# A first attention layer that turns its weights in one block, projects values later, and scores with high and low parts of q and k

## The reference, cut to what matters

```python
for i in range(DEPTH):                       # DEPTH = 2
    if i < N_A:  mix = conformer_conv(x, ...)               # layer 0
    else:                                                   # layer 1
        k_shared, v_shared = x @ kv_wk, x @ kv_wv           # 16 heads of 64
        q = x @ b_wq[j]
        mix = stick_breaking_attention(q, k_shared, v_shared) @ b_wo[j]
    x = layer_norm(DN_ALPHA * x + mix, ln_mix_g[i], ln_mix_b[i])
    ffn = conv_gated_ffn(x, ...)
    ple = jax.nn.sigmoid(x @ ple_w_gate[i]) * (p[i] @ ple_w_proj[i])
    x = layer_norm(DN_ALPHA * x + ffn + ple, ln_ffn_g[i], ln_ffn_b[i])

def stick_breaking_attention(q, k, v):       # per head and block of 128 queries
    z = einsum('bhqd,bhkd->bhqk', qblk, kh) * scale
    log_1m = where(mask, log_sigmoid(-z), 0.0)              # mask: key before query
    rev = cumsum(log_1m, axis=3, reverse=True)
    a = where(mask, exp(log_sigmoid(z) + (rev - log_1m)), 0.0)
    return einsum('bhqk,bhkd->bhqd', a, vh)
```

## Time and profile before

| | |
|---|---|
| median of 3 runs | 2419.19 us (2417.32 to 2421.7) |
| the profiled execution's own time | 2417.3 us |
| its span in the profile | 2415.5 us |
| PE busy | 2356.6 us (98% of the span) |
| PEld / DVE / ACT / POOL busy | 79% / 38% / 40% / 40% |
| granted TensorE clock over the span | 0.997 of full |

### The profile page before, as it was taken

How to read it: one execution, slowest core, us unless ns; L and a number is a source line. 1 busy time by engine, 2 the same in 40 slices (tenths; PEclk the granted TensorE clock), 3 DMA queues, 4 the chain that set the end, 5 groups by cost and what they waited for, 6 DMA issues and landing times.

```text
span 2415.5 us, 30601 instructions
## 1 busy us (share of the span) xinstructions
PE 2356.6 (98%) x11320; PEld 1912.9 (79%) x11320; DVE 912.2 (38%) x1167; ACT 950.2 (39%) x1612; POOL 955.9 (40%) x422
## 2 busy tenths in 40 slices
PE   8989999999999999999999999999999989999998
PEld 6858888888877778888888888888877658888887
DVE  6985344420343323544400422210556862232201
ACT  7764333322454434433322522221534564322222
POOL 5834444444422223444444344444322103444443
PEclk9999999999999999999999999999999999999999
DMA  5212322222212122322222223223312002322222
GB/s 184 70 40 95 119 96 96 96 96 96 88 53 68 64 79 88 113 97 98 99 92 92 89 99 98 96 92 100 146 64 69 28 1 79 105 96 96 96 96 96
DMA packets 58755, 215.17 MB, mean 89 GB/s; under 512 B 6448, under 2 KB 6448, under 8 KB 58416
## 3 DMA queue, kind: packets, MB, share of 16 engines
q1 hardware_dynamic: 55440, 199.83, 24.7%
q10 hardware_dynamic: 3232, 14.16, 1.6%
HBM read 211.86 MB, written 2.10 MB: 89 GB/s over the span
## 4 chain that ended last, share of the span: by engine, by line
PE 87%; DVE 7%; ACT 3%; issue 2%; DMA 1%; SPq 0%; POOL 0%; DVEq 0%; ACTq 0%; POOLq 0%
PE banks L458 17%; PE banks L459 17%; PE banks L460 17%; PE banks L484 9%; PE banks L486 9%; PE banks L485 9%; DVE banks L1708 3%; PE banks L495 1%; PE banks L857 1%; PE banks L730 1%; PE banks L752 1%; PE banks L900 1%; ACT tmp L1473 1%; DMA raw<-ws 1%; PE banks L812 0%
## 5 line engine op out<-in xcount | busy, mean ns | idle before, releaser
L416 POOL TENSOR_TENSOR wL<-raw,wH 128x1024 fp32r<-128x1024 f32 x369 | 892.8, 2421 | 1423.3 <-ACT wH L1053 1423.1
L1053 ACT ACTIVATE wH<-raw 128x1024 fp32r<-128x1024 f32 x371 | 393.2, 1060 | 1108.8 <-PE banks L460 607.1
L458 PE MATMUL banks<-xH,wH 128*128 128x512 f32 (+1 forms) x1976 | 762.7, 386 | 13.3 <-DVE xL L1552 10.8
L459 PE MATMUL banks<-xL,wH 128*128 128x512 f32 (+1 forms) x1976 | 756.2, 383 | 0.0
L460 PE MATMUL banks<-xH,wL 128*128 128x512 f32 (+1 forms) x1976 | 756.1, 383 | 0.0
L458 PEld LDWEIGHTS banks<-xH,wH 128*128 128x128 f32 x1976 | 371.7, 188 | 93.7 <-DVE wL L1557 10.8
L460 PEld LDWEIGHTS banks<-xH,wL 128*128 128x128 f32 x1976 | 371.8, 188 | 72.8
L459 PEld LDWEIGHTS banks<-xL,wH 128*128 128x128 f32 x1976 | 371.9, 188 | 71.5 <-issue 0.7
L484 PE MATMUL banks<-wH,hH 128*128 128x512 f32 x704 | 274.2, 389 | 3.5 <-DVE tmp L1666 3.5
L486 PE MATMUL banks<-wL,hH 128*128 128x512 f32 x704 | 273.9, 389 | 0.0
L485 PE MATMUL banks<-wH,hL 128*128 128x512 f32 x704 | 273.9, 389 | 0.0
(11 more groups left out here) (247 smaller groups left out, 2275.1 us busy)
## 6 DMA issues: line engine op xcount, KB each, us to landing
raw<-ws SPq DMA_DIRECT2D x371, 512.0 KB, 3.6
w1b<-w ACTq DMA_DIRECT2D x2, 2048.0 KB, 11.4
tmp<-rows ACTq DMA_DIRECT2D x7, 512.0 KB, 3.3
b_row<-rows ACTq DMA_DIRECT2D x5, 512.0 KB, 4.4
tmp<-xT SPq DMA_DIRECT2D x8, 256.0 KB, 7.4
xr<-xN ACTq DMA_DIRECT2D x1, 2048.0 KB, 8.6
out<-xr SPq DMA_DIRECT2D x4, 512.0 KB, 2.6
pf<-pT ACTq DMA_DIRECT2D x2, 512.0 KB, 3.8
```

The costliest lines, as they stand in the source:

```text
L416: pool.tensor_tensor(wL[:, j, :], raw[:, j, :], fp(wH[:, j, :]), ALU.subtract).then_inc(low_ready, 1)
L458: pe.matmul(bank, wH[:, slot, cols], rh, start=start, stop=False)
L459: pe.matmul(bank, wH[:, slot, cols], rl, start=False, stop=False)
L1053: act.activation(wH[:, c % SLOTS, :], raw[:, c % SLOTS, :], ACT.Copy).then_inc(high_ready, 1)
```

## The change

q and k are kept as high and low parts (`qH`, `qL`, `kH`, `kL`, one buffer each, where `qT` and `kT` had two). ACT's copies now write `qH` and `kH`; DVE gets two new operations per pair, `low_queries` and `low_keys`, each a 128x512 pass over a PSUM bank, with a new semaphore `qk_low`. A score tile is now three fp32r products, and in `scores` all masks come first and all score tiles after them. On PE the three `turn_weights` follow each other, `project(p+1, 2)` comes after them, and `turn_values(p+1)` after `values(p)`; ACT's order follows. In the stage after the mixer of both layers ACT divides `xg` itself (`divide_block`), PE turns it with a transpose, and DVE's `finish_block` becomes `shift_block`, which only adds the shift row. ACT's order in `mix_norm` changes too.

```diff
             def turn_block(xname, q, src):
...
-                    mm = pe.matmul(bank[:, o:o + P], src(q)[:, n * P:n * P + P], turner[:, q, :], start=True, stop=True)
+                    if src is divided:
+                        mm = pe.transpose(bank[:, o:o + P], xg[:, q, n * P:n * P + P], cc("ident"))
+                    else:
+                        mm = pe.matmul(bank[:, o:o + P], src(q)[:, n * P:n * P + P], turner[:, q, :], start=True, stop=True)
...
             def project(p, j, which):
                 if which != 1 and p:
                     pe.wait_ge(q_free, p * 4 + (which + 1))
+                    pe.wait_ge(qk_low, 2 * p + which // 2)
...
             def turn_values(p, j):
                 pe.wait_ge(qkv_copied, p * 4 + 3)
+                pe.wait_ge(qk_low, p * 2 + 1)
...
             def scores(p, j):
+                if p:
+                    pe.wait_ge(bT_ready, 3 * p)
                 for n, tiles in enumerate(PARTS3):
-                    if p:
-                        pe.wait_ge(bT_ready, 3 * (p - 1) + n + 1)
                     for h in range(2):
                         for i, (qt, o, w) in enumerate(tiles):
                             pe.matmul(ps[2 * n + h][:, o + w - P:o + w], maskSB, identB, start=i == 0, stop=False,
                                       skip_group_check=True)
-                    if n == 0:
-                        pe.wait_ge(qkv_copied, p * 4 + 2)
+                pe.wait_ge(qk_low, p * 2 + 2)
+                for n, tiles in enumerate(PARTS3):
                     for i, (qt, o, w) in enumerate(tiles):
-                        for h in range(2):
-                            r = slice(DH * h, DH * h + DH)
-                            mm = pe.matmul(ps[2 * n + h][:, o:o + w], qT[r, j, qt * P:qt * P + P], kT[r, j, 0:w],
-                                           start=False, stop=False, skip_group_check=True)
...
+                        for q, k in ((qH, kH), (qH, kL), (qL, kH)):
+                            for h in range(2):
+                                r = slice(DH * h, DH * h + DH)
+                                mm = pe.matmul(ps[2 * n + h][:, o:o + w], q[r, qt * P:qt * P + P], k[r, 0:w],
+                                               start=False, stop=False, skip_group_check=True)
...
@@ pair, on PE
-                    turn_weights(p, 0)
+                    for n in range(3):
+                        turn_weights(p, n)
                     project(p + 1, 1 - j, 2)
-                    turn_weights(p, 1)
-                    turn_weights(p, 2)
-                    turn_values(p + 1, 1 - j)
...
                 pe.wait_ge(qkv_copied, p * 4 + 4)
+                if more:
+                    pe.wait_ge(qk_low, 2 * p + 4)
                 values(p, j)
+                if more:
+                    turn_values(p + 1, 1 - j)
...
@@ on ACT
+            def divide_block(name, q):
+                deviation(name, q)
+                act.wait_ge(x_centred, QT * LN_OF[name] + q + 1)
+                act.activation(xg[:, q, :], xg[:, q, :], ACT.Copy, scale=figure(name, q, 4)).then_inc(x_normed, 1)
...
@@ mix_norm
-                for q in range(QT):
-                    unit_block(name, q)
+                for q in range(3):
+                    divide_block(name, q)
+                keep(0)
+                divide_block(name, 3)
+                keep(1)
                 high_after(c0 - 1)
-                keep(0)
-                high_tiles(xname, 0, 0, 2, shift=f"mix_b{layer}")
-                keep(1)
-                high(c0 + LEAD)
-                high_tiles(xname, 0, 2, 4, shift=f"mix_b{layer}")
+                high_tiles(xname, 0, 0, 4, shift=f"mix_b{layer}")
                 keep(2)
                 keep(3)
+                high(c0 + LEAD)
                 high_tiles(xname, 1, 0, 4, shift=f"mix_b{layer}")
...
@@ pair, on ACT
-                copy_weights(p, 0)
+                for n in range(3):
+                    copy_weights(p, n)
                 if more:
                     copy_qkv(p + 1, 1 - j, 2)
-                copy_weights(p, 1)
-                copy_weights(p, 2)
-                if more:
-                    copy_values(p + 1, 1 - j)
                 act.wait_ge(av_ready, p * 2 + 2)
                 act.activation(mH[:, bass.ds(p, 1), :].rearrange("p o t -> p (o t)"), ps[6][:], ACT.Copy)\
                     .then_inc(m_high, 1)
+                if more:
+                    copy_values(p + 1, 1 - j)
...
@@ on DVE
+            def shift_block(xname, q):
+                dve.wait_ge(x_normed, QT * TURN[xname] + q + 1)
+                dve.tensor_tensor(xr[:, q, :], xg[:, q, :], b_row[:], ALU.add).then_inc(res_step, 1)
...
+            def low_queries(p):
+                dve.wait_ge(qkv_copied, p * 4 + 1)
+                dve.scalar_tensor_tensor(qL[:], ps[7], DH ** -0.5, fp(qH[:]), ALU.mult, ALU.subtract).then_inc(qk_low, 1)
+
+            def low_keys(p):
+                dve.wait_ge(qkv_copied, p * 4 + 2)
+                dve.tensor_tensor(kL[:], ps[6], fp(kH[:]), ALU.subtract).then_inc(qk_low, 1)
...
@@ pair, on DVE: between the last weigh and the wait for m_high
+                if more:
+                    low_queries(p + 1)
+                    low_keys(p + 1)
```

More of the change, by code:

```diff
@@ L167, in build_block @@
             ("dwL", [P, KT * CONV_W], F32)])
-        (mH, mL, qT, kT, vT, vN, beta, bT) = overlay([
-            ("mH", [P, KT, S], F32R), ("mL", [P, KT, S], F32R), ("qT", [P, 2, S], F32), ("kT", [P, 2, S], F32),
+        (mH, mL, qH, qL, kH, kL, vT, vN, beta, bT) = overlay([
+            ("mH", [P, KT, S], F32R), ("mL", [P, KT, S], F32R), ("qH", [P, S], F32R), ("qL", [P, S], F32R),
+            ("kH", [P, S], F32R), ("kL", [P, S], F32R),
             ("vT", [P, S], F32), ("vN", [P, 2, QT, P], F32),
@@ L283, in build_block @@
         bT_ready = sem("bT_ready")
+        qk_low = sem("qk_low")
         av_ready = sem("av_ready")
@@ L506, in updated, with divided @@
                 return xr[:, q, :]
+            def divided(q):
+                return xg[:, q, :]
             def first_chunks(outs, c, name, xname, src, turn_at, fill):
@@ L630, in ple @@
                 pe.wait_ge(block_taken, 8 * full + 8)
-                src = centred(("pw2", "wo")[layer])
-                turn_block(xname, 0, src)
-                turn_block(xname, 1, src)
+                turn_block(xname, 0, divided)
+                turn_block(xname, 1, divided)
                 for q in range(2, QT):
@@ L639, in ple @@
                 pe.wait_ge(x_ready, XV[xname] + KT)
-                turn_block(xname, 2, src)
-                turn_block(xname, 3, src)
+                turn_block(xname, 2, divided)
+                turn_block(xname, 3, divided)
                 def gate(k, qs, last=False):
@@ L724, in scores @@
                                       skip_group_check=True)
-                    if n == 0:
-                        pe.wait_ge(qkv_copied, p * 4 + 2)
+                pe.wait_ge(qk_low, p * 2 + 2)
+                for n, tiles in enumerate(PARTS3):
                     for i, (qt, o, w) in enumerate(tiles):
-                        for h in range(2):
-                            r = slice(DH * h, DH * h + DH)
-                            mm = pe.matmul(ps[2 * n + h][:, o:o + w], qT[r, j, qt * P:qt * P + P], kT[r, j, 0:w],
-                                           start=False, stop=False, skip_group_check=True)
-                            if i == len(tiles) - 1:
-                                mm.then_inc(z_ready, 1)
+                        for q, k in ((qH, kH), (qH, kL), (qL, kH)):
[3 more added lines that the diff above has]
+                                               start=False, stop=False, skip_group_check=True)
+                                if i == len(tiles) - 1 and q is qL:
+                                    mm.then_inc(z_ready, 1)
             def turn_weights(p, n):
@@ L1304, in copy_qkv @@
                 if which == 0:
-                    act.activation(qT[:, j, :], ps[7][:], ACT.Copy, scale=DH ** -0.5).then_inc(qkv_copied, 1)
+                    act.activation(qH[:], ps[7][:], ACT.Copy, scale=DH ** -0.5).then_inc(qkv_copied, 1)
                 elif which == 1:
-                    act.activation(kT[:, j, :], ps[6][:], ACT.Copy).then_inc(qkv_copied, 1)
+                    act.activation(kH[:], ps[6][:], ACT.Copy).then_inc(qkv_copied, 1)
                 else:
@@ L1733, in _ @@
             for q in range(QT):
-                finish_block("pw2", q)
+                shift_block("mix0", q)
             ple(0)
@@ L1763, in weigh, with pair @@
                     .then_inc(a_ready, 1)
-            def pair(p):
+            def low_queries(p):
[4 more added lines that the diff above has]
+                dve.tensor_tensor(kL[:], ps[6], fp(kH[:]), ALU.subtract).then_inc(qk_low, 1)
+            def pair(p, more=True):
                 for n, tiles in enumerate(PARTS3):
@@ L1778, in _ @@
             dve.wait_ge(zero_ready, 1)
```

(7 more changed lines are left out.)

## The result

The kernel after took 2396.99 us (median of four runs, 2395.74 to 2399.52) against 2418.26 us for the kernel before (four runs, 2416.87 to 2421.7): 0.9911 of the time, interval 0.9894 to 0.9928. The forecast was 2397.0. The profiled execution of after is the slowest of its four, 2399.52 us.

What follows compares the result with a forecast made beforehand. PE, busy 98% of the span, bounds the kernel. Seven pairs 15.4, last pair 0.9 and mixers 5.6 sum to 21.9 us, taking the profiled 2417.3 to 2395.4, a median of 2397 us; range 2391 to 2410.

Steps and rivals of the forecast that it cites:

- Order, 1.32 per pair: PE's order in a pair: transposes of weights before v, of v after values; gain 1.98 - 0.54 - 0.12 = 1.32 us.
- Scores, 0.88: Masks and scores of a pair: fp32r products with heads side by side, masks together; 2.64 us against 3.52, gain 0.88.
- the loss of about a quarter: Score products: four row tiles only 3.07 times as fast as one; some 0.6 us more per pair, 4.9 in all.
- New work on DVE costs nothing: DVE's two low-part passes per pair, about 0.7 us each, covered by 3 us or more; cost 0.
- The last pair gains only its scores: Last attention pair, without v or the old wait: gains 0.9 us, if its small matmuls hide DVE as now.
- After each mixer, 2.8 per layer: Stage after each mixer: transposes replace fp32 turns, less a 0.85 us wait for low tiles; 2.8 us per layer, 5.6 in all.
- Heads in turn: Rival in the scores: heads run one after another in fp32r, 15.2 us less gain, 2412 us; chance 0.12.
- Another wait in the old one's place: Rival before the values: v's copy, `low_keys` or a late `wH` holds PE; 10 us, 2407 us; chance 0.08.
- Turns bring nothing: Rival after the mixers: ACT's longer chain holds PE as long as the turns save; 2403 us; chance 0.06.
- Slow products: Rival in the scores: 64-row products go at the fp32 pace, 5.2 us more per pair; 2439 us; chance 0.05.
- Clock: Rival at v: clock falls to 1.2 GHz after twenty transposes together, 36 us more; 2433 us; chance 0.02.
- PE is what counts, and the pair's period the place: Whole kernel: only what PE executes or waits for counts; a pair falls from 26.61 to 24.41 us, seven pairs 15.4.

Runs made afterwards that it cites:

- a2: Kernel before with only the new scores and low parts, old order and old mixer stage: 2409.48 us (0.9966).
- b2: Kernel after with each part's masks put back just before its score tiles: 2402.84 us (0.9928 of before).
- b4: Kernel after with three extra scratch passes on DVE before each of the two low parts: 2397.16 us (0.9903 of before).
- c1: Kernel after, block 2's transposes after the mixer waiting only for the low tiles in their own bank: 2397.56 us (0.9909 of before).
- d2: Kernel after with each of DVE's four shift passes after both mixers done twice: 2410.57 us (0.9966 of before).
- b3: Kernel after with v's transposes and ACT's copy of them ahead of the values again: 2403.52 us (0.993 of before).
- a3: Kernel before with only the new stage after the mixers (ACT divides, PE transposes, DVE adds the shift): 2413.74 us (0.9979).
- b1: Kernel after with head 0's three score products queued before head 1's, instead of alternating: 2396.99 us (0.9903 of before).

## Why the prediction was right, and where it was not

- *PE is what counts, and the pair's period the place.* Right. Attention gives 17.5 of the 21.9 us.
- *Order, 1.32 per pair.* Right in its mechanism, and it gave 1.51. The copies are hidden by v as argued, v's transposes cost 0.49 (0.54 foreseen) and the drain before the values 0.09 (0.12). What was left out is 0.11: twenty transposes in one block have one uncovered weight load less than eight and twelve, 2.10 against 2.21.
- *Scores, 0.88.* Beside the new order it is 0.86, alone in a2 0.79. Masks and scores took 2.66 against 2.64 foreseen. The heads run side by side with no loss in fp32r; the loss of about a quarter that the prediction set beside it did not occur. But the prediction gave one number for two things, and b2 shows that the masks' place is the larger part: 0.56 us of it.
- *New work on DVE costs nothing.* Right: the low parts are ready within 0.1 us of the times worked out (12.6 and 15.2 us into the pair), and b4 shows that PE doesn't wait for them.
- *The last pair gains only its scores.* Not contradicted: 17.51 - 7 x 2.37 = 0.9.
- *After each mixer, 2.8 per layer.* This term was mis-sized: 2.2. The turns save what was forecast: 3.49 us become 1.66 in the first group, 1.83 less (the prediction had 3.57 for the old group, 0.08 more than its starts give, and 1.75 for the new one). The wait was too small: ACT takes 2.97 us per block, not 2.9, and sat idle 0.41 before the third division, so the tiles start 0.5 us later than worked out, and the wait costs 1.38 us by starts rather than 0.85. The wait is the one named.
- *What covers the rest.* The prediction named the gate product's second chunk as just covered; in after its `wL` is ready 0.4 us before PE starts it, and c1 confirms that little is left. It missed the third: `shift_block` was costed at nothing as "a pass of the same width", which holds for DVE but not for POOL, whose pass beside it grows from 3.49 us in before to 6.85. It was hidden by 0.3 us. This was the thinnest part of the forecast, and d2 shows the price beyond it.
- *The sum.* 16.3 for attention against 17.5 measured, 5.6 for the mixers against 4.4: the two errors of 1.2 cancelled. The forecast's closeness to the median is partly luck; its two stages were each right to 1.2 us. The base moved as well: the forecast started from 2419.19, and the median beside the result was 2418.26.
- *The range.* Its lower end allows 3.4 us for the mixer's wait in two layers. The forecast charged 0.85 per layer, so without the wait it is 1.7 better and not 3.4; the measured time doesn't come near that end.
- *The rivals.* Heads in turn: no, 3 ns apart. Another wait in the old one's place: not in after, but b3 shows it when the values are turned first. Turns bring nothing: a3 excludes it. Slow products: the pace was 0.23 us at 512 columns and 0.11 to 0.12 at 128 and 256. Clock: 1.00 over the seven pairs, with twenty transposes together.

## What to carry to other kernels

When PE waits for a copy of what it has just turned, look for the large product that doesn't need the copy and put it between; then check what stands in the old place, since the next short turn leaves the same wait (b3). Instructions that change how many rows of the array are used are worth grouping: here the place of eight small masks was worth more than the faster products. When a pass is moved or made shorter on DVE, ask what POOL does at that time: a pass costed at nothing on DVE can lengthen POOL's by as much as all of DVE's row, as in after and d2, though it does not always.

## What the runs showed of the hardware that was not expected

- Two 64-row products of different rows start within 10 ns of each other even with two other products of the first head between them in the program (b1).
- Each change between 128-row and 64-row instructions cost about 0.14 us on average (b2, 4.5 us over eight pairs and four changes).
- A POOL pass of 2.40 us lasted 3.49, 6.85 or 11.32 us beside one (before), four (after) or eight (d2) DVE passes with two inputs from SBUF, while in the last two cases DVE's own took 1.22 each, undisturbed. At 184 us of after, beside another row of four, POOL's pass took 3.38 and two of DVE's took 3.41.
- After a wait of 4.2 us of PE in each layer (d2) its products started 0.43 us apart for the next 6 us, at a granted clock of 0.50, and the stretch of 70 us around it was granted 0.95; with the wait of 1.2 us in after it was granted 1.00.
